# Up pages of experts 8 to 29 asked for by ScalarE, and another order of the last two experts

## What is computed

```python
# top-1 of 4 groups, then top-2 of the group's 8 experts: 32 experts a layer
hb = jax.nn.silu(xb @ w_gate[e]) * (xb @ w_up[e])     # 1024 -> 512, twice
return hb @ w_down[e]                                  # 512 -> 1024
# each token's two outputs, weighted by its gates, are added to the residual
```

## Time and profile before

| | |
|---|---|
| median of 3 runs | 1268.96 us (1267.98 to 1270.03) |
| the profiled execution | 1268.41 us, its span 1266.7 us |
| busy share of the span | TensorE 82%, its weight loads 56%, VectorE 38%, ScalarE 19% |
| transfers | 461.49 MB, mean 364 GB/s |
| mean granted TensorE clock | 0.902 |

### The profile page before, as it was taken

How to read it: one execution, slowest core, us unless ns; L and a number is a source line. 1 busy time by engine, 2 the same in 40 slices (tenths; PEclk the granted TensorE clock), 3 DMA queues, 4 the chain that set the end, 5 groups by cost and what they waited for, 6 DMA issues and landing times.

```text
span 1266.7 us, 22370 instructions
## 1 busy us (share of the span) xinstructions
PE 1040.9 (82%) x9525; PEld 704.6 (56%) x9525; DVE 478.3 (38%) x1230; ACT 234.8 (19%) x526; POOL 4.9 (0%) x27
## 2 busy tenths in 40 slices
PE   9999998866767575889999999999967675758676
PEld 7888755533433342448888888876533333425243
DVE  2342543532223222237665556464343222222223
ACT  2221121111111111103433333121111111111111
POOL 1000000000000000000000000000000000000000
PEclk9999998978788877899999999999988878878789
DMA  9888799999999999996676664899999999999997
GB/s 342 237 338 332 255 419 429 426 428 428 429 429 428 429 429 427 417 394 187 190 231 225 229 223 151 334 361 427 428 427 427 430 428 429 427 429 429 429 419 297
DMA packets 98305, 461.49 MB, mean 364 GB/s; under 512 B 17468, under 2 KB 60728, under 8 KB 73400
## 3 DMA queue, kind: packets, MB, share of 16 engines
q1 hardware_dynamic: 97872, 460.34, 90.5%
q10 hardware_dynamic: 360, 0.15, 0.0%
HBM read 459.38 MB, written 1.08 MB: 364 GB/s over the span
## 4 chain that ended last, share of the span: by engine, by line
PE 51%; DMA 45%; SPq 1%; DVE 1%; issue 1%; ACT 1%; POOL 0%; POOLq 0%; DVEq 0%; ACTq 0%
DMA front<-in_expert_w_up 39%; PE pa L1534 10%; PE pa L1829 8%; PE pb L1534 8%; DMA arena<-in_expert_w_down 5%; PE wa L1829 5%; PE acc L1565 4%; PE wb L1859 3%; PE acc L1684 2%; PE pb L1609 1%; SPq L362 1%; PE pb L1903 1%; PE wa L2124 1%; PE pb L1785 1%; PE acc L1869 1%
## 5 line engine op out<-in xcount | busy, mean ns | idle before, releaser
L1829 PE MATMUL pa<-front,arena 128*32 128x256 f32 x1792 | 126.6, 445 | 80.8 <-DMA front<-in_expert_w_up 80.8
L1289 DVE TENSOR_SCALAR lower<-lower 128x128 f32<-128x128 f32 x64 | 14.4, 225 | 417.6 <-ACT lower L606 417.6
L1829 PE MATMUL wa<-front,arena 128*32 128x256 f32 x1232 | 96.7, 479 | 88.5 <-DMA front<-in_expert_w_up 85.0
L1829 PEld LDWEIGHTS pa<-front,arena 128*32 128x32 f32 x1792 | 63.0, 128 | 146.9 <-DMA front<-in_expert_w_up 93.6
L1829 PEld LDWEIGHTS wa<-front,arena 128*32 128x32 f32 x1232 | 46.1, 136 | 142.1 <-DMA front<-in_expert_w_up 95.0
L606 ACT ACTIVATE arena<-wb 32x256 f32<-32x256 f32 (+2 forms) x236 | 88.9, 377 | 105.0 <-PE wb L1859 96.6
L1859 PE MATMUL wb<-w_dn,conv_raw 128*32 128x256 f32 x1472 | 87.9, 379 | 2.3 <-DMA w_dn<-in_expert_w_down 2.0
L1534 PE MATMUL pa<-hnT,w_x 128*128 128x256 f32 x384 | 85.1, 380 | 0.0
L1829 PE MATMUL wa<-w_x,arena 128*32 128x256 f32 x896 | 64.4, 451 | 19.1 <-DMA w_x<-in_expert_w_up 19.1
L1534 PEld LDWEIGHTS pa<-hnT,w_x 128*128 128x128 f32 x384 | 72.5, 190 | 10.0 <-issue 0.3
L1534 PE MATMUL pb<-hnT,w_x 128*128 128x256 f32 x336 | 74.5, 380 | 0.0
(11 more groups left out here) (345 smaller groups left out, 1252.0 us busy)
## 6 DMA issues: line engine op xcount, KB each, us to landing
w_dn<-in_expert_w_down SPq DMA_DIRECT2D x46, 2048.0 KB, 26.4
front<-in_expert_w_gate SPq DMA_DIRECT2D x42, 2048.0 KB, 19.1
front<-in_expert_w_up SPq DMA_DIRECT2D x42, 2048.0 KB, 23.6
w_x<-in_expert_w_gate SPq DMA_DIRECT2D x15, 2048.0 KB, 32.2
w_x<-in_expert_w_up SPq DMA_DIRECT2D x15, 2048.0 KB, 36.6
arena<-in_expert_w_down SPq DMA_DIRECT2D x14, 2048.0 KB, 25.8
w_x<-in_odd_in_proj SPq DMA_DIRECT2D x16, 1024.0 KB, 5.5
front<-in_expert_w_up SPq DMA_DIRECT2D x10, 1024.0 KB, 8.8
```

The lines of the kernel that those rows point to most:

```text
L1289: link(v.tensor_scalar(eg, eg, 1.0, None, ALU.add))
L1829: ins = mm(gu[32 * j:32 * j + 32, :, :], xb[:, k, c0:c0 + CAP], w[k][:, :, P * j:P * j + P], start=(k == 0), stop=(k == KC - 1))
```

## The change

ScalarE gets a function `up_page(l, e)`, called behind the exponential of expert e (and behind the copies of expert e - 1). It asks, on ScalarE's own queue, for the up page of each expert from 8 to 29 whose predecessor in the buffer is e. SyncE leaves these out. At the layer's end SyncE asks for the down page of 30 ahead of the overflow check, then for gate and up of 30, then for gate and up of 31 in halves (the first halves count to `gu_res`), and last for the down page of 31. TensorE works the down products of 30 right behind the gate and up products of 30, and those of 31 in two halves of the contraction, each behind its own wait; `warm(6)` is gone. ScalarE's copy of expert 30 stands ahead of the exponential of 31. The wait for `dn_in3b` before the load of the final norm is gone. In the diff `act`, `sp_` and `pe` are ScalarE, SyncE and TensorE.

```diff
@@ -32,6 +32,7 @@
 SLOT = [0, 1, 2, 0, 1, 2, 0, 1] + [2, 0, 1, 0] * len(LOOP) + [1, 2, 0, 1]
 DSLOT = [0, 1, 2, 3, 4, 0, 1, 2] + [4, 0, 1, 2] * len(LOOP) + [4, 0, 1, 3]
 PRE = 5
+OWN = 2 * QUAD
 WIDE = 5
 FIRST = 4
 RELEASES = 5
@@ -436,16 +437,24 @@
                 sp_.wait_ge(S["order_done"], l + 1)
                 for e in range(PRE, NE - 2):
                     which = expert_at(l, e)
-                    for part in (2, 0, 1):
+                    for part in (2, 0, 1) if e < OWN else (2, 0):
                         expert_part(l, e, part, NE * l + previous(DSLOT if part == 2 else SLOT, e), which)
                 last = [(e, expert_at(l, e)) for e in (NE - 2, NE - 1)]
+                expert_part(l, NE - 2, 2, NE * l + previous(DSLOT, NE - 2), last[0][1])
                 overflow_weights(l)
                 k1 = sp_.value_load(table[0:1, l + 1:l + 2], min_val=0, max_val=OV_LIST)
                 sp_.wait_ge(S["ov_done"], k1 + 1)
-                for parts in ((0, 1), (2,)):
-                    for e, which in last:
-                        for part in parts:
-                            expert_part(l, e, part, NE * l + previous(DSLOT if part == 2 else SLOT, e), which)
+                for part in range(2):
+                    expert_part(l, NE - 2, part, NE * l + previous(SLOT, NE - 2), last[0][1])
+                sp_.wait_ge(S["gu_done"], NE * l + previous(SLOT, NE - 1) + 1)
+                for half in range(2):
+                    k = slice(KC // 2 * half, KC // 2 * half + KC // 2)
+                    for part in range(2):
+                        w = (expert_w_gate, expert_w_up)[part][l, ds(last[1][1], 1), :, :]
+                        sp_.dma_start(w_gu[SLOT[NE - 1]][:, part, k, :],
+                                      w.rearrange("a (p k) f -> p (a k) f", k=KC)[:, k, :]
+                                      ).then_inc(S[("gu_res", "gu_in1")[half]], 16)
+                expert_part(l, NE - 1, 2, NE * l + previous(DSLOT, NE - 1), last[1][1])
 
             def late_params():
                 sp_.dma_start(nffn[:, :, :], norm_ffn.rearrange("l (p k) -> p l k", k=KC)).then_inc(S["par_wr"], 16)
@@ -550,7 +559,6 @@
             expert_part(1, 2, 1)
             expert_stream(1)
             sp_.wait_ge(S["gu_done"], 2 * NE - 2)
-            sp_.wait_ge(S["dn_in3b"], 2 * uses(DSLOT, 3, NE) * 16)
             sp_.dma_start(fnorm, final_norm.partition_broadcast(P)).then_inc(S["fnorm_in"], 16)
             for t, i, sem, n in ((0, 0, "sum_sq", 5), (0, 1, "y_ready", 3), (1, 0, "sum_sq", 6), (1, 1, "y_ready", 4)):
                 sp_.wait_ge(S[sem], n)
@@ -728,6 +736,14 @@
                     ins = af(yq[r, (c + j) % 4, :], Y_ps[r, :], ACT.Copy)
                 ins.then_inc(S["y_copied"], 1)
 
+            def up_page(l, before):
+                for e in range(OWN, NE - 2):
+                    if previous(SLOT, e) == before:
+                        which = act.value_load(order[0:1, NE * l + e:NE * l + e + 1], min_val=0, max_val=NE - 1)
+                        w = expert_w_up[l, ds(which, 1), :, :].rearrange("a (p k) f -> p (a k) f", k=KC)
+                        act.dma_start(w_gu[SLOT[e]][:, 1], w).then_inc(
+                            (S["gu_in0"], S["gu_in1"], S["gu_in2"])[SLOT[e]], 16)
+
             def overflow(k):
                 act.wait_ge(S["ov_gu"], k + 1)
                 af(o_eg, GU[0][:, 0, :], ACT.Exp, scale=-1.0).then_inc(S["ov_act"], 1)
@@ -759,11 +775,12 @@
                     if e == NE - 3:
                         output_alone(l, e - 1)
                         output_alone(l, e)
-                    if e == NE - 1:
-                        output_alone(l, e - 1)
+                    if e == NE - 2:
+                        output_alone(l, e)
                     if e == WIDE:
                         act.wait_ge(S["w_gu"], l + 1)
                         af(o_eg, GU[0][:, 0, :], ACT.Exp, scale=-1.0).then_inc(S["w_act"], 1)
+                    up_page(l, e)
                     if e == WIDE + 1:
                         act.wait_ge(S["w_dn"], l + 1)
                         af(o_y, Y_ps, ACT.Copy).then_inc(S["w_act"], 1)
@@ -1970,16 +1987,21 @@
                                 middle_quad(l, q)
                         continue
                     s = SLOT[e]
+                    if e == NE - 1:
+                        pe.wait_ge(S["gu_res"], 48 * l + 48)
+                        gate_up(xs, CAP * j, gu_cols(s), GU[e % 2], ks=range(KC // 2))
                     pe.wait_ge((S["gu_in0"], S["gu_in1"], S["gu_in2"])[s], (uses(SLOT, s, NE) * l + uses(SLOT, s, e + 1)) * 32
                                + (112 * (l + 1) + 16 * (l + (e >= 3)), 48 * l + (16, 48)[e >= 4], 32)[s])
                     if e == 3:
-                        pe.wait_ge(S["gu_res"], 16 * l + 16)
+                        pe.wait_ge(S["gu_res"], 48 * l + 16)
                     if e == WIDE:
                         pe.wait_ge(S["w_vec"], 3 * l + 2)
                     if e == WIDE + 1:
                         pe.wait_ge(S["w_vec"], 3 * l + 3)
                     if e == 0:
                         first_gate_up(l)
+                    elif e == NE - 1:
+                        gate_up(xs, CAP * j, gu_cols(s), GU[e % 2], ks=range(KC // 2, KC)).then_inc(S["gu_done"], 1)
                     else:
                         w = early_cols(e) if e == 1 else late_cols(e) if e in (3, 4) else gu_cols(s)
                         gate_up(xs, CAP * j, w, GU[e % 2], PARTS * l + FIRST + 2 * q if j == 0 else None,
@@ -1988,7 +2010,7 @@
                         positions(l)
                     if e == 2:
                         rows_of(1, l)
-                    if e and e != NE - 2:
+                    if e and e < NE - 2:
                         down_of(l, e - 1)
                     if e == WIDE:
                         second_passes(l)
@@ -2008,7 +2030,7 @@
                         rows_of(e + 1, l)
                         sum_alone(l, e - 1)
                     if e == NE - 2:
-                        warm(6)
+                        down_of(l, e)
                     if e == WIDE + 1:
                         second_down(l)
                     if j == 0 and q and e != WIDE - 1:
```

## The result

| | kernel before | changed kernel |
|---|---|---|
| median, beside one another on one chip | 1269.14 us (7 runs, 1266.91 to 1271.27) | 1275.33 us (7 runs, 1271.41 to 1276.45) |
| the profiled execution | 1268.41 us, span 1266.7 | 1273.61 us, span 1271.9 |
| mean granted TensorE clock | 0.902 | 0.891 |

The two medians alone lie 6.2 us apart, inside that interval. One execution of each kernel was traced, and a trace shows that one: the changed kernel's took 1273.61 us, 1.7 less than its median. The prediction had +4.3 us, 1273.3, in a range of 1266.5 to 1280.

The account below looks back on a forecast made before the run. Transfers at 425 to 430 GB/s were taken to bound the kernel, with TensorE setting the layers' ends after the change. Layer 1's +3.5 and layer 0's +0.8 gave +4.3 on 1268.96: 1273.3 us, range 1266.5 to 1280.

Parts of the forecast that it names:

- expert 28 a page late: Near each layer's end: expert 29's up page, asked for early, makes expert 28 start one page, 4.9 us, later.
- the length of the last chain: Layer's end: from expert 30's start through 31's last down product, one unbroken TensorE chain of 16.8 us.
- layer 1's term: End of layer 1: TensorE's late start and new chain end the last down product 3.5 us later.
- The rate, the number of ScalarE's requests, the halves, the final norm: 0: Stream and small edits: each worth nothing, the earlier final norm load 0 to 0.1 us.
- changing queues costs: Rival, in the stream: each of 44 pages costs about 0.4 us of an engine, +18 us, 1291; chance 0.08.
- a second queue raises the rate: Rival, in the stream: a second queue fills seams between packets, 1% giving -6.9 + 4.3, 1266.4; chance 0.13.
- Expert 27 late by 7.6: Near each layer's end: 1.55 pages go ahead at half the engines, so expert 27 starts 7.6 us later.
- Expert 28 unbroken and at the high clock: Near each layer's end: no idle time ahead of expert 28, so its 64 products take 3.66 us at 2.4 GHz.
- cold and late: Rival: expert 28 runs at 1.2 GHz, +1.7 us in layer 1 and +2.4 in layer 0, 1277.4; chance 0.13.
- Layer 0's term: End of layer 0: +0.8 us, taken between +0.2 and +1.3 depending on the check's idle time.
- Down page of 30 ahead of the check: 0: Layer's end: SyncE's earlier request fills its queue where nothing had run dry, worth 0.
- the bytes stay the bound: Rival: ScalarE's pages displace none, only the new tail counts, +0.9 us, 1269.9; chance 0.18.

Follow-up runs that it names:

- i: Kernel before, with the up pages of experts 8 to 28 asked for by ScalarE, 29's left to SyncE, old end; ratio 0.9994 (0.9985 to 1.0003).
- k: Kernel before, with products of zeros ahead of expert 28 and the check, and no wait ahead of the final norm's load; ratio 0.9997 (0.9987 to 1.0007).
- d: Kernel before, with expert 29's up page alone asked for by ScalarE, old end; ratio 1.0059 (1.0045 to 1.0072).
- g: Changed kernel plus ten products of zeros ahead of expert 28's products; ratio to the kernel before 1.0023 (1.0014 to 1.0033).
- l: Changed kernel plus ten products of zeros ahead of expert 28 and eight ahead of the check; ratio to the kernel before 1.0016 (1.0004 to 1.0028).
- j: Kernel before, with only the request for the down page of 30 moved ahead of the overflow check; ratio 1.0034 (1.0021 to 1.0047).
- b: Changed kernel with all up pages asked for by SyncE as before, new end kept; ratio to the kernel before 1.0040 (1.0026 to 1.0055).
- a: Kernel before, with up pages of experts 8 to 29 asked for by ScalarE, old end; ratio 1.0053 (1.0036 to 1.0071).
- c: Changed kernel with expert 29's up page given back to SyncE; ratio to the kernel before 1.0039 (1.0024 to 1.0053).
- e: Changed kernel with TensorE's old order of the last two experts; ratio to the kernel before 1.0035 (1.0020 to 1.0049).
- f: Changed kernel with TensorE's old order of the last two experts and expert 29's up page by SyncE; ratio to the kernel before 1.0034 (1.0022 to 1.0046).
- h: b plus ten products of zeros ahead of expert 30's products; ratio to the kernel before 1.0014 (1.0002 to 1.0025).

## Why the prediction was right, and where its reasons were not

The time and its sign were right, the two rivals on rate and queues fell, and three of the steps held: nothing for the second queue, expert 28 a page late, and the length of the last chain. The other reasons did not hold, and that the sum came within 0.6 us is in part luck: layer 1's term was 2.1 us too small and layer 0's 0.8 too large.

- **The rate, the number of ScalarE's requests, the halves, the final norm: 0.** i has 42 of the 44 moved requests and stands at -0.8 us (-1.9 to +0.4), k has the early norm load beside its products of zeros and stands at -0.4. In i "changing queues costs" would be some +17 us (42 times 0.4) and "a second queue raises the rate" -6.9, and both are excluded. (The share of 2.7% by which the prediction argued against the first is that of 3 to 5 us, not of 4 to 5.) The requests in halves were not tried alone.
- **Expert 28 a page late, +4.9.** Measured from the stage's first products: 379.3 against 374.2 in layer 0 (+5.1), 380.3 against 374.2 in layer 1 (+6.0). d, with 378.9 and 379.4, shows that the one page of expert 29 does it.
- **Expert 27 late by 7.6: failed.** It was 5.1 and 6.0 late. The half share was right; the time of the request was not. The step took 14.69 us between the products of 26 and 27. But 26 had itself become later by two pages (354.2 against 344.8, +9.4; in layer 1 +9.7), so 27 followed it after 10.35 and 10.95 us, and 28's page was asked for 2.5 us ahead of 27's start (507.90 and 510.39), with its first packets only 3 us behind the request. None of it had passed.
- **Expert 28 unbroken and at the high clock: failed, as a consequence.** TensorE had 2.81 and 2.79 us to wait, and the 64 products took 6.51 and 5.24 us. The window from 525 to 530 us shows a granted clock of 0.50, the 1.2 GHz level:

```profile
525.00:530.00 5.00, 4.93 (x48) 2.37 (x52) 0.00 (x0) 0.00 (x0) 0.00 (x0) 0.50 1.02 433
```

This was the rival "cold and late", which had +8.4. Its clock came true, but its price did not add up in layer 0. g and l show what the clock is worth in the whole kernel: 2.0 and 2.9 us.
- **Layer 1's term, +3.5: too small.** It measured +5.6. Expert 28 started 0.6 us later than the sum had it (380.3 against 379.6 into the stage), and was 1.6 us slower (5.24 against 3.66); together they are nearly all of the missing 2.1. The chain from expert 30's start to the end was worked out as 16.8 us and measured 1262.24 - 1245.44 = 16.8.
- **Layer 0's term, +0.8: too large.** It measured 0.0. 28 was 2.9 us dearer, but from its end to the start of 29 passed 7.0 us instead of the 9.7 of the sum. The sum had 2.39 us of idle time for the check there; none stood ahead of 29, and 1.21 us inside its products, behind the check. That this came out so near to 28's extra 2.9 us, and layer 0 at 0.0, is luck.
- **"Down page of 30 ahead of the check: 0": the step that was wrong in kind.** j, which is that request alone, costs 4.3 us, as much as the whole change within the error of either, though not by the same path: in the changed kernel 30 finds its page there. The step looked whether a queue runs dry. It didn't ask which pages move back by one and how much TensorE still has to do behind them (8.9 us behind a page that is one page from the end). For the same reason the rival "the bytes stay the bound" was mis-sized: b is its case, with +5.1 instead of +0.9. Expert 30 started close to where it said (1244.16 - 839.99 = 404.2 us into the stage against 403.6), but behind idle time and so at the low clock: the chain was 18.8 us (to 1262.99), not 16.8.
- **Adding the parts: right only by cover.** The sum put the loss on the page of 29, with the new end as its price. The sum had none of the second cause. The runs show two, each enough by itself: with the old order of requests the page of 29 costs 6.7 to 7.5 us (a, d), with the new one any form without products of zeros costs 4.3 to 5.1 (b, c, e, f, j and the changed kernel). In the changed kernel the late 28 hides the wait of 30 (its line has no bracket), and the down page of 30 fills the queue where d runs dry: layer 0 ends 2.8 us late in d and on time in the changed kernel. TensorE's new order by itself isn't measurably dearer than the old (changed against e, 0.5 us).

Products of zeros give back 2.9 us (0.8 to 5.1) of the changed kernel's 4.9 (l), so about that much is low clock. The rest, 2.0, isn't divided: l's trace still has expert 30 at 6.24 us behind a wait of 3.06, so part of the rest is low clock as well, and part is later pages. Why 28's products are at the high clock in some executions and not in others stays open, and so does what ends the idle time ahead of 29.

## What to carry to other kernels

When the transfers never stop, asking for a page early is not free: it is paid by the page that would have gone in its place. Where TensorE doesn't need that page sooner it costs nothing (21 of the 22 pages here); where it does, the price is that page's lateness, less the slack behind it, and the low clock that can follow the wait. At the end of such a stream, count for each page how many stand behind it and how much work stands behind its use; here two pages (9.8 us) behind the last gate and up pages covered 8.9 us of work and one page (4.9 us) did not, so that moving one request turned an end set by bytes into one set by work. Time two parts of a change alone before their costs are added, since here each of two losses hid the other.

## What the runs showed of the hardware that had not been expected

Between ScalarE's request (507.90) and the first packets of its queue lay some 3 us, though the engines were busy throughout with the other queue (101.3% of them from 508 to 511); then it had half at once. And an idle time of only 2 to 3 us ahead of a block of 64 products could make it 5.0 to 6.5 us instead of 3.66, which can be as much again as the wait itself (2.85 us behind 2.81 in layer 0); ten products of zeros in that wait (2.33 us) took it away in every trace of g, h, k and l. The length of the idle time alone doesn't decide it: j's expert 31 took 3.66 us behind 2.80, and b's 28 took 3.66 behind 1.63, where the kernel before had 5.35 behind 2.18.
